# Halving a weight unit in place: the low half takes the raw unit's buffer, and the raw unit is fetched when its slot is used up

## What is computed

```python
def first_block(x, ...):                    # 2 layers
    for l in range(DEPTH):
        proj = rms_norm(x, attn_norm[l]) @ w_in[l]                  # three attentions' inputs
        o_mla, o_diff, o_ch = mla(...), diff(...), chunk(...)       # 6 + 6 + 4 heads, normed
        x = x + jnp.concatenate([o_mla, o_diff, o_ch], axis=-1) @ w_out[l]
        x = x + conv_ffn(rms_norm(x, ffn_norm[l]), w_ffn_in[l], ..., w_ffn_out[l])   # d_ff 2816
    return rms_norm(x, final_norm)

def second_block(x, p, ...):                # 2 layers
    for i in range(DEPTH):
        h = mixer(x, ..., w_in[i], w_branch_a[i], w_branch_b[i], w_out[i])           # two attentions, gated
        x = layer_norm(ALPHA * x + h, ...)
        mlp = square(relu(x @ w_up[i])) @ w_down[i]                                  # d_ff 4096
        ple = sigmoid(x @ w_ple_gate[i] + b_ple_gate[i]) * (p[i] @ w_ple[i])
        x = layer_norm(ALPHA * x + mlp + ple, ...)
    return x
```

## Time and profile before

| | before |
|---|---|
| median of three timed runs | 2973.92 us |
| profiled execution, first to last instruction (span) | 2967.3 us |
| granted TensorE clock, mean | 0.994 of full speed |
| TensorE busy with matmuls | 2910.2 us, 98% |
| VectorE, ScalarE, GpSimd busy | 46%, 28%, 46% |
| splits on GpSimd (L531) | 460, 2406 ns each |
| raw loads, high loads | 460 each of 512 KB, 3.5 and 4.1 us median from issue to landing |
| DMA queue of the raw loads, of the high loads | 25.6% and 26.4% of the 16 DMA engines' span |

### The profile page before, as it was taken

One profiled execution on the slowest core, in us unless ns is written; L12 is line 12 of the kernel. 1 busy time (PEld: TensorE's weight loads), 2 busy tenths in 40 slices (PEclk: granted clock), 3 DMA queues, 4 the chain that ended last, 5 costly groups with the idle time before them and its releaser, 6 DMA issues.

```text
span 2967.3 us, 40814 instructions
## 1 busy us (share of the span) xinstructions
PE 2910.2 (98%) x14054; PEld 2397.7 (81%) x14054; DVE 1376.6 (46%) x3151; ACT 838.6 (28%) x1881; POOL 1364.1 (46%) x924
## 2 busy tenths in 40 slices
PE   7999999999999999999999999999999999999998
PEld 6778888888778888879888878888798888788886
DVE  6487525254576524255773541111547734411124
ACT  3354312122363212122553231001325532300012
POOL 4222555564213555555333645555453335455552
PEclk9999999999999999999999999999999999999999
DMA  7323666665324665656334756656463337565663
GB/s 253 108 87 106 186 196 192 192 212 170 107 72 133 198 191 183 205 185 199 114 116 128 224 165 195 194 182 206 146 199 114 114 121 222 168 193 190 192 199 106
DMA packets 136521, 494.16 MB, mean 167 GB/s; under 512 B 15280, under 2 KB 15536, under 8 KB 136112
## 3 DMA queue, kind: packets, MB, share of 16 engines
q0 software_dynamic: 66240, 241.20, 26.4%
q1 hardware_dynamic: 68544, 245.40, 25.6%
q10 hardware_dynamic: 1584, 5.46, 0.5%
HBM read 489.91 MB, written 2.10 MB: 166 GB/s over the span
## 4 chain that ended last, share of the span: by engine, by line
PE 95%; DVE 2%; ACT 2%; issue 1%; DMA 1%; POOL 0%; SPq 0%; POOLq 0%; DVEq 0%; ACTq 0%
PE ps L558 26%; PE ps L560 25%; PE ps L559 25%; PE ps L744 3%; PE ps L767 2%; PE ps L815 2%; PE ps L693 1%; PE ps L695 1%; PE ps L694 1%; PE ps L757 1%; PE ps L807 1%; PE ps L796 1%; PE ps L797 1%; PE ps L629 0%; PE ps L1038 0%
## 5 line engine op out<-in xcount | busy, mean ns | idle before, releaser
L558 PE MATMUL ps<-hi,w_hi 128*128 128x512 f32 x3216 | 1271.1, 395 | 9.0 <-DVE lo L1602 5.3
L560 PE MATMUL ps<-lo,w_hi 128*128 128x512 f32 x3216 | 1255.9, 391 | 0.0
L559 PE MATMUL ps<-hi,w_lo 128*128 128x512 f32 x3216 | 1255.7, 390 | 0.0
L531 POOL TENSOR_TENSOR w_lo<-w_raw,w_hi 128x1024 fp32r<-128x1024 f32 x460 | 1106.5, 2406 | 102.9 <-DMA w_hi<-weights 93.4
L526 POOL DMA_DIRECT2D w_hi<-weights x460 | 261.4, 568 | 1464.2 <-PE ps L560 1324.9
L558 PEld LDWEIGHTS ps<-hi,w_hi 128*128 128x128 f32 x3216 | 605.6, 188 | 160.5 <-issue 25.6
L560 PEld LDWEIGHTS ps<-lo,w_hi 128*128 128x128 f32 x3216 | 605.3, 188 | 128.8
L559 PEld LDWEIGHTS ps<-hi,w_lo 128*128 128x128 f32 x3216 | 606.2, 188 | 118.2 <-issue 1.0
L1728 DVE SCALAR_TENSOR_TENSOR x<-x,ps 128x512 f32<-128x512 f32 x64 | 43.9, 687 | 287.1 <-PE ps L560 287.1
L1985 ACT ACTIVATE ps<-hb,col 128x512 f32<-128x512 f32 x88 | 68.6, 782 | 381.1 <-DVE hb L1172 381.1
L2123 ACT ACTIVATE sq<-ps 128x512 f32<-128x512 f32 x64 | 38.2, 597 | 465.5 <-PE ps L560 465.5
(11 more groups left out here) (345 smaller groups left out, 3209.2 us busy)
## 6 DMA issues: line engine op xcount, KB each, us to landing
w_raw<-weights SPq DMA_DIRECT2D x460, 512.0 KB, 3.5
w_hi<-weights POOLq DMA_DIRECT2D x460, 512.0 KB, 4.1
x<-xt SPq DMA_DIRECT2D x8, 256.0 KB, 10.1
out<-x SPq DMA_DIRECT2D x8, 256.0 KB, 2.0
kc<-k ACTq DMA_DIRECT2D x1, 1346.0 KB, 5.7
bias<-relb ACTq DMA_DIRECT2D x2, 512.0 KB, 4.9
bias<-relb ACTq DMA_DIRECT2D x1, 1024.0 KB, 4.8
praw<-pt ACTq DMA_DIRECT2D x2, 512.0 KB, 5.9
```

The source lines that it names most:

```text
L531: nc.gpsimd.tensor_tensor(wlo[s][:, :], raw[s][:, :], whi[s][:, :].bitcast(F32), ALU.subtract).then_inc(w_split, 1)
L558: nc.tensor.matmul(out_ap, w[0], xx[0], start=first, stop=False)
L559: nc.tensor.matmul(out_ap, w[1], xx[0], start=False, stop=False)
L560: return nc.tensor.matmul(out_ap, w[0], xx[1], start=False, stop=last)
```

## The change

The low half gets the address of the raw unit in its slot, so that the split reads `w_raw` and writes its result over it; the four separate `w_lo` buffers go (16 KB a partition, which nothing else takes up). The raw unit can then be fetched only when the low half that lies there has been used, so SP waits for `w_used` where it waited for `w_split`. The order of the instructions on each engine stays as it is.

```diff
-        raw = [place(f"w_raw{i}", [P, UNIT], F32, take(4096)) for i in range(RING)]
+        raw_at = [take(4096) for _ in range(RING)]
+        raw = [place(f"w_raw{i}", [P, UNIT], F32, raw_at[i]) for i in range(RING)]
         whi = [place(f"w_hi{i}", [P, UNIT], F32R, take(4096)) for i in range(RING)]
-        wlo = [place(f"w_lo{i}", [P, UNIT], F32R, take(4096)) for i in range(RING)]
+        wlo = [place(f"w_lo{i}", [P, UNIT], F32R, raw_at[i]) for i in range(RING)]
...
             with sp.Fori(1, N_UNITS // RING) as i:
                 for s in range(RING):
-                    sp.wait_ge(w_split, i * RING + (s + 1 - RING))
+                    sp.wait_ge(w_used, i * RING + (s + 1 - RING))
                     sp.dma_start(raw[s][:, :], weights[i * RING + s]).then_inc(w_loaded[s], 16)
```

## The result

Over 20 timed runs each, the changed kernel takes 2978.95 us (2970.4 to 2981.58) and the one before 2972.97 us (2969.43 to 2975.96): a ratio of 1.0017, 95% interval 1.0011 to 1.0023. Two further timings gave 1.0021 and 1.0018. The change costs some 5 to 6 us, where 1.0 us of gain was forecast. Three timed runs could not have told so small a difference; twenty of each can. The time lies inside the forecast range, but the direction was wrong.

What follows compares the result with a forecast made beforehand. TensorE was taken to bound the kernel. All terms were 0 but -1.0 us at unit 100, so the timed 2973.92 us became 2972.9 us; range 2968 to 2980.5 us.

Steps and rivals of the forecast that it cites:

- What bounds the kernel: Whole kernel: TensorE is 95% of the chain that ended last; the change can lose time only by making units late.
- the dense stretches: Weight stream at 5.44 us a unit: GpSimd's order hides the delayed raw load by 2.1 us, cost 0.
- Rivals 5 and 6: 5: loads late in dense stretches too, +210 us, chance 0.02. 6: nothing moves, lead spare everywhere, 2973.9 us, chance 0.12.
- The split in place: GpSimd's split writing over its input: no change in its time (2.41 us usual), cost 0.
- Rival 4: GpSimd's splits: a split in place is dearer, 2.92 us each, +3.0 us, 2976.9 us, chance 0.05.
- what changes is what meets: Fast stretches, unit 100: raw load gets a head start, high load meets less, 4.5 instead of 5.0 us; -1.0 us taken.
- The wait of 1.93 us would be gone: TensorE before unit 100: with high loads at 4.5 us its split comes earlier and the wait goes; middle, -1.0 us, taken.
- rival 2: Unit 100: the wait goes with its clock dip, -1.9 - 1.7 = -3.6 us, 2970.3 us, chance 0.14.
- Rival 1: Fast stretches, units 100, 248, 379: loads meet, landing time T 6.2 us, decides from 5.7; +7.8 us, 2981.7 us, chance 0.10.
- The start-up: First units and VectorE's chain to TensorE's 4.2 us wait: gain 0, bounds -3.9 and +2.4 us.
- Rival 3: Unit 100's wait goes and the start-up's chain slips out from behind the last split: -9.2 us, 2964.7 us, chance 0.05.
- A wait can also cost clock: After unit 100's 1.93 us wait TensorE's clock halves for 3.4 us, 1.7 us of work lost; kept in the forecast.

Runs made afterwards that it cites:

- late_only: Kernel before with only the wait changed to `w_used`, the separate `w_lo` buffers kept: 2976.65 us, 1.0018 of the kernel before.
- dec_halfraw: Late fetch, separate low-half buffers, dec_before's ScalarE exchange; raw loads after the first four bring half their columns, so results are wrong: 2968.4 us, 0.9984.
- dec pairs: Kernel before and changed kernel, both with dec_before's ScalarE exchange, timed twice: 2968.34 against 2973.11 us, then 2968.88 against 2974.13 us.
- ring5: Changed kernel with five slots instead of four and TensorE's loops over groups of four units written out: 2969.77 us, 0.9994 of the kernel before.
- dec_ring5: ring5 with dec_before's exchange on ScalarE: 2968.86 us, 0.9984 of the kernel before.
- metered: Changed kernel, SP's loop unrolled, raw load of unit n+4 also waiting for the split of unit n+2: 2972.89 us, 1.0010 of the kernel before.
- one_early: Kernel before, separate buffers, raw load of unit n+4 waiting for split of n and use of n-1: 2976.24 us, 1.0002.
- dec_later: dec_after with each raw load let go one unit later still: 3030.74 us, 1.0201 of the kernel before, over five runs.
- dec_before: Kernel before with an exchange on ScalarE: in the first layer it empties TensorE's value banks ahead of the table work: 2968.34 us, 0.9981.
- dec_before2: dec_before word for word again: 2968.88 us, 0.9979 of the kernel before.
- dec_after: Changed kernel with dec_before's exchange on ScalarE: 2973.11 us, 1.0002 of the kernel before.
- dec_after2: dec_after again, paired with dec_before2: 2974.13 us, 1.0000 of the kernel before.
- unrolled4: Changed kernel with four slots and TensorE's loops written out as in ring5, as its control: 2975.22 us, 1.0000 of the kernel before.

## Why the prediction was wrong

**What bounds the kernel, and the dense stretches: right.** Splits start 0.59 us behind their high load, nothing waits for `w_raw`, high loads take 4.3 to 4.8 us where 4 to 5 was given; raw loads stayed at 3.3, better than the 3.8 to 4.5 given. Rivals 5 and 6 (a late feeder everywhere, nothing moves) did not come.

**The split in place: right,** 2408 against 2406 ns, and late_only loses as much without it. Rival 4 falls.

**The step that failed** is the one on "what changes is what meets": "the raw load then has a head start and the high load meets less. With high loads at 4.5 us instead of 5.0 ... I take the middle, -1.0 us." The high load meets more. Its median rose from 4.1 to 4.7 us over the program, stayed at 5.0 from 644 to 672 us and reached 6.6. The reasoning took one raw load 0.4 us ahead of one high load, which is the middle of a group. At a group's head two units come free within a microsecond, and since SP now waits for the same event as GpSimd, both raw loads start around the one high load that the next split needs. Before, the wait on `w_split` had fetched those raw units earlier, and the high load had the DMA engines nearly to itself, 3.6 us. The lead in time was spare; the spacing that the old wait gave as a by-product was not. dec_halfraw beside the two dec pairs shows it: with fewer bytes there the waits and the loss are gone. ring5 and dec_ring5 agree, with the reserve about the written-out loops. metered only moves the wait to the next unit, and one_early leaves it where it is.

**The same term had a second gap.** "The wait of 1.93 us would be gone" looked at the split alone. TensorE also waits there for the last chunk of the activations, through VectorE's residual step (L1328) and ScalarE's rounding (L1785) that follows: with the split early, 0.98 us (ring5, dec_ring5) and 1.02 (dec_halfraw) are left. At most about 1 us of the 1.93 was to be had, and rival 2's 3.6 us with it were out of reach. A smaller slip: the split of 2.35 us, given as of rows 7, stands in rows 9.

**Rival 1 had the mechanism,** two raw loads beside one high load at a group's head, with T at 6.2. In the changed kernel's profiles, with and without the exchange on ScalarE, 5.8 to 8.1 us were measured, and its point of decision, 5.7, is within 0.1 us of the 5.6 to 5.7 measured. That is not luck: the high load and the split have two units' time, 8.2 us, in the rule and in the trace. It had 0.10 and deserved the first place. Its places were partly off: it looked where the trace of before already waited (unit 100: 1.93 before, 1.25 to 2.62 in the changed kernel's executions) and at units 248 and 379, which wait at most 0.23 us in all but dec_later. The waits came at units 95 and 194, which are fetched at the head of a group with 18 matmuls a unit and of which the trace of before had shown nothing, since their high loads landed early. Its own price for one such place, 2.0 us and a clock fall of 1.7, lies above most of the 0.24 to 2.44 us of wait measured at unit 95 and 0.41 to 2.16 at unit 194.

**Weighing the page.** The Trainium skill's "DMA: Bandwidth & Descriptors" (section Bandwidth) gives 6.15 us for 1 MB in one transfer, and I set it aside for the start-up's 405 GB/s. At the group's head 1.5 MB take from 644.13 to 651.4, 7.3 us; in the dense stretch the two loads of a unit take 5.2 (SP's issue at 380.97 to the landing of the high load of 381.44, 4.76 us after its own issue). By the page's figure, as an estimate, that would be 9.2 and 6.15: both too high, and the two loads take twice the 2.6 us that I worked out from 405 GB/s. The page was the better guide, though its figure is for one transfer and these are two and three.

**The start-up: the term 0 was right for the change, with bounds too narrow.** L693's wait of 4.20 us became 4.97 in the first profile and 0.7 to 7.6 in others with the late fetch, 3.4 longer at most where the bound was 2.4. Taking TensorE off that chain gains both kernels 4 to 6 us and leaves the change's cost at 4.8 and 5.3. Rival 3's idea of such a gain was real, but needed an edit of its own.

**Clock.** "A wait can also cost clock" is borne out only in size: about 1 us of the loss by the timed runs' clocks.

**What stays open.** In the profiled executions TensorE's waits for splits grow by 2 to 4 us (dec_before 2.7 and dec_before2 2.9 in all, dec_after 4.7, dec_after2 7.1), the timed runs differ by 4.8 and 5.3, of which 4.8 and 4.2 are not clock. So the waits seen for splits grew by 1.9 us against a loss of 4.8 in the first pair, and by 4.2 against 4.2 in the second, some of it at units where the change can't be told from chance. And the profiled spans of the dec pairs, set to full clock, lie within about 1 us of each other, the changed kernel's not even the longer, and unrolled4 and one_early, at 1.0000 and 1.0002, lose nothing that can be told beside their waits. A profiled execution is one draw out of a spread as wide as the effect. That the raw loads' bytes beside the high load make TensorE wait is shown; that they are all of the 5 us is not.

**A better version.** dec_before, with the old wait, is at 0.9981 and 0.9979 faster than both kernels. dec_ring5, at 0.9984, is as fast within the noise, with the split in place, the late fetch and 8 KB a partition less than before.

## What to carry to other kernels

When a prefetch is let go by a later event, ask not only whether it still arrives in time but what else that event, and the ones within a microsecond of it, let go: the early wait may have been what kept two streams apart. Look for it where units come free in pairs, not where the trace of before already waits; there the lead that the collision eats is invisible. And take a noisy coupling out of both kernels before measuring 5 us between them.

## What the runs showed of the hardware

- Two 512 KB raw loads and one 512 KB high load within 0.9 us land after 3.3, 6.4 and 6.6 us, against 3.2 to 3.4 (raw) and 3.5 to 3.8 (high) alone. The raw load that starts first is hardly slowed, here and in the dense stretch (3.3), and the high load behind it pays (4.4 beside one, 6.6 beside two). All DMA engines together moved 260 GB/s there in the mean of 644 to 660 us and 381 at the most (646 to 648), 405 in the start-up. Halving the raw loads' bytes brings the high load to 5.3.
- A split that writes over its input takes as long as one that doesn't.
- The granted clock's falls to 0.50 in attention differ between executions of one kernel in number and in length (3.4 or 6.8 us). Span times one less the mean granted clock is 25.0 to 27.5 us a run in the mean for the kernels before and after, and 21 to 24 for those with the exchange on ScalarE.
- VectorE steps of 0.42 us are held to the end of a GpSimd split when it starts first; a shift of a few tenths of a microsecond between the two decides about 2.6 us of VectorE's chain (3.83 against 1.27). The Trainium skill's "SBUF — State Buffer" (section Who interferes with whom) has the rule that the one of the two engines that comes second is blocked for the whole instruction of the other. The trace agrees; that the winner changes between executions is what these runs add.
